# A decoder block's expert layer: 160 instead of 128 of 512 tokens by gathered rows, 352 instead of 384 by dense products

## The reference

```python
def peer_ffn(xn, wq, sub_keys, u, v):          # xn: 512 tokens x 2048
    q = (xt @ wq).reshape(t, 8, 2, 128)        # 8 heads, two half keys
    sc = einsum('thpc,hpnc->thpn', q, sub_keys)
    top_v, top_i = lax.top_k(sc, 16)           # per half key
    ...                                        # best 16 of the 16 x 16 pairs
    expert = take_along_axis(cand_id, best_pos)   # 16 of 16384 experts per head
    gate = softmax(best_v)
    hc = einsum('cd,chkd->chk', xc, u[ec])     # one dot product per chosen expert
    ac = gc * gelu(hc)
    return einsum('chk,chkd->cd', ac, v[ec])   # weighted sum of rows of v
```

## Time and profile before

| what | value |
| --- | --- |
| runs | 3308.53, 3305.33, 6432.45 us; median 3308.53 us |
| profiled execution | 3301.1 us, of which the span from first to last instruction 3299.3 us |
| granted TensorE clock, mean | 0.988 |
| groups of stage 3 | about 1189 to 3076 us of the span |

### The profile page before, as it was taken

How to read it: one execution, slowest core, us unless ns; L and a number is a source line. 1 busy time by engine, 2 the same in 40 slices (tenths; PEclk the granted TensorE clock), 3 DMA queues, 4 the chain that set the end, 5 groups by cost and what they waited for, 6 DMA issues and landing times.

```text
span 3299.3 us, 46895 instructions
## 1 busy us (share of the span) xinstructions
PE 3180.3 (96%) x17074; PEld 2965.8 (90%) x17074; DVE 2431.3 (74%) x3461; ACT 1078.1 (33%) x1379; POOL 659.4 (20%) x464
## 2 busy tenths in 40 slices
PE   7999999999997879999999999999999999999997
PEld 5777778899997779999999999999999999999785
DVE  6544443599977968888887888888888888885644
ACT  4224422222233533333333333333332333333422
POOL 3120000066673111112111121111212111110200
PEclk9999999999998999999999999999999999999998
DMA  4243122344566668888788887888878788863322
GB/s 147 81 153 111 67 84 94 105 112 112 114 187 216 232 238 286 291 285 302 266 291 287 279 306 265 293 282 279 302 270 297 277 286 291 283 238 117 102 90 100
DMA packets 249394, 694.46 MB, mean 210 GB/s; under 512 B 35824, under 2 KB 93680, under 8 KB 213360
## 3 DMA queue, kind: packets, MB, share of 16 engines
q1 hardware_dynamic: 189424, 418.77, 37.0%
q0 software_dynamic: 55296, 268.53, 24.0%
q10 hardware_dynamic: 4608, 6.29, 0.5%
HBM read 657.79 MB, written 35.72 MB: 210 GB/s over the span
## 4 chain that ended last, share of the span: by engine, by line
PE 73%; DVE 16%; DMA 4%; issue 4%; ACT 2%; POOL 1%; DVEq 0%; SPq 0%; ACTq 0%
PE bank L486 23%; PE bank L488 23%; PE bank L487 23%; DVE w_lo L1203 4%; DMA raw<-in_u_t 3%; DVE one_ij L1548 2%; DMA raw<-in_v 1%; ACT w_hi L875 1%; DVE row L1526 1%; PE bank L578 1%; PE bank L601 1%; PE bank L579 1%; POOL gate_matrix L1790 1%; DVE x_lo L1659 1%; DVE x_lo L1220 1%
## 5 line engine op out<-in xcount | busy, mean ns | idle before, releaser
L486 PE MATMUL bank<-x_hi,w_hi 128*128 128x384 f32 (+1 forms) x3024 | 1079.8, 357 | 35.8 <-DVE x_lo L1220 16.7
L488 PE MATMUL bank<-x_hi,w_lo 128*128 128x384 f32 (+1 forms) x3024 | 1069.9, 354 | 0.0
L487 PE MATMUL bank<-x_lo,w_hi 128*128 128x384 f32 (+1 forms) x3024 | 1069.8, 354 | 0.0
L875 ACT ACTIVATE w_hi<-raw 128x1024 fp32r<-128x1024 f32 (+1 forms) x668 | 688.3, 1049 | 887.7 <-DMA raw<-in_v 336.7
L1203 DVE TENSOR_TENSOR w_lo<-raw,w_hi 128x1024 fp32r<-128x1024 f32 (+1 forms) x668 | 802.9, 1219 | 210.0 <-ACT w_hi L875 200.3
L486 PE MATMUL bank<-a_hi,w_hi 128*128 128x384 f32 x2048 | 687.6, 336 | 14.3 <-DVE w_lo L1203 11.1
L487 PE MATMUL bank<-a_lo,w_hi 128*128 128x384 f32 x2048 | 685.8, 335 | 0.0
L488 PE MATMUL bank<-a_hi,w_lo 128*128 128x384 f32 x2048 | 685.8, 335 | 0.0
L486 PEld LDWEIGHTS bank<-x_hi,w_hi 128*128 128x128 f32 x3024 | 571.4, 189 | 85.4 <-DVE w_lo L1203 16.8
L487 PEld LDWEIGHTS bank<-x_lo,w_hi 128*128 128x128 f32 x3024 | 571.9, 189 | 38.8 <-issue 1.2
L488 PEld LDWEIGHTS bank<-x_hi,w_lo 128*128 128x128 f32 x3024 | 571.0, 189 | 38.9
(11 more groups left out here) (198 smaller groups left out, 2049.5 us busy)
## 6 DMA issues: line engine op xcount, KB each, us to landing
raw<-in_u_t SPq DMA_DIRECT2D x256, 512.0 KB
raw<-in_v SPq DMA_DIRECT2D x256, 512.0 KB
g_tile<-gate_matrix SPq DMA_DIRECT2D x32, 768.0 KB
raw<-in_w_o SPq DMA_DIRECT2D x32, 512.0 KB
raw<-in_w_q SPq DMA_DIRECT2D x32, 512.0 KB
gate_matrix<-g_blk SPq DMA_DIRECT2D x8, 2048.0 KB, 7.4
raw<-in_w_gate SPq DMA_DIRECT2D x32, 512.0 KB
raw<-in_w_in SPq DMA_DIRECT2D x26, 512.0 KB
```

The lines of the kernel that those rows point to most:

```text
L486: pe.matmul(out, w_hi[slot][:, blk, :], m_hi, start=first, stop=False)
L487: pe.matmul(out, w_hi[slot][:, blk, :], m_lo, start=False, stop=False)
L488: return pe.matmul(out, w_lo[slot][:, blk, :], m_hi, start=False, stop=last)
L875: act.activation(w_hi[slot][:, 8 * s:8 * s + n, :], raw[s][:, 0:n, :], ACT.Copy)\
```

## The change

TD becomes 352 and the unit of tokens in `x2_hi` and `x2_lo` becomes 32 instead of 128 (TK), so that dense products read 11 pieces of 32 tokens instead of 3 of 128. Tokens 352 to 383 get row buffers of another shape: 32 tokens are spread over the partitions four times, and each copy takes two of the eight heads, so 32 loads of 1 MB bring their rows of `u` and 32 those of `v`. There are 160 dots and 160 mixes in place of 128 each (ALL_ROWS). ALONE becomes 12, ONE_TB 7. Per group there are 12 rows in groups 0 and 1, and 10 (PER_G) in all others up to 29; the added ones stand at the end of quarters 1 and 3 (of all four quarters in groups 0 and 1).

`row_acc` now is the memory of `x_rows`, and so is cleared, by POOL, only when all dots are done. The activations for the rows are made from `h` by ACT and transposed by PE (`rows_stage`, `sparse_rows`) after the first unit of the ALONE stage; those of the spread tokens are made in group 0. At the end 16 small matmuls with a `fold` matrix add the four copies.

```diff
-TD = 384
-TCD = TD // P
+TD = 352
+TCD = TD // P + 1
+TK = 32
-ALONE = 11
+ALONE = 12
-PER_G = 8
-G_DOT = (ROWS - EARLY) // PER_G
+PER_G = 10
+ROWS_B = TK
+ALL_ROWS = ROWS + ROWS_B
+G_DOT = (ALL_ROWS - EARLY) // PER_G
-        x2_hi = at("x2_hi", two, [P, TC, DC, P], F32R)
+        x2_hi = at("x2_hi", two, [P, NPC, DC, TK], F32R)
-        row_acc = at("row_acc", one + 35 * K, [P, D])
+        row_acc = x_rows
+        x_rows_b = at("x_rows_b", one + 35 * K, [P, D])
+        row_acc_b = x_rows_b
...
+        def b_parts(g):
+            return range(4) if g < 2 else (1, 3)
...
             def sparse_rows(i):
-                    pe.matmul(out, x2_hi[:, TCD, 4 * i + j, :], ident_r[:, :], start=True, stop=False)
-                    mm = pe.matmul(out, x2_lo[:, TCD, 4 * i + j, :], ident_r[:, :], start=False, stop=True)
+                for n in (2 * i, 2 * i + 1):
+                    pe.wait_ge(stage_ready, n + 1)
...
+                        mm = pe.transpose(bank[6 + i % 2][:, k * P:(k + 1) * P], stage[n % 2][:, j, :], ident[:, :])
+            def fold_acc_b():
+                pe.wait_ge(acc_added, 3)
+                for c in range(DC):
+                    mm = pe.matmul(bank[6][:, c * TK:(c + 1) * TK], row_acc_b[:, c * P:(c + 1) * P], fold[:, :],
+                                   start=True, stop=True)
...
                 if e == 5:
...
+                    act.wait_ge(topk_step, PER_TOPK * PH)
+                    for q in range(4):
+                        act.dma_start(expert_b[ts, :], ...).then_inc(expert_b_in, 16)
+                        act.dma_start(gate_rows_b[ts, :], ...).then_inc(expert_b_in, 16)
...
             def peer_group(g, par, first=False, last=False):      # ACT
                 if first:
                     hi(peer_unit(g, 1), peer_slot(1, par))
+                    rows_stage_b(0)
+                    rows_stage_b(1)
...
+                    rows_evict_b(0)
+                    rows_evict_b(1)
+                    rows_stage_b(2)
+                    rows_stage_b(3)
...
                 dve.scalar_tensor_tensor(of_head(expert), i_of[:, TCD, :], float(NK), j_of[:, TCD, :], ...)
+                dve.scalar_tensor_tensor(of_head(expert_c), i_of[:, TCD - 1, :], float(NK), j_of[:, TCD - 1, :], ...)
...
                         if c == 1:                                # DVE, quarter q of a group
                             rows(3 + q)
+                        if c == 3:
+                            rows_b(q)
...
-            dve.memset(row_acc[:, :], 0.0).then_inc(acc_zero, 1)
...
-            for k in range(EARLY, 2 * ROWS):                      # POOL
-                load_row(k)
+            for g in range(G_DOT):
+                load_group(g, EARLY + 8 * g, 4 * g if g < 2 else 4 + 2 * g, u_rows)
+            pool.wait_ge(row_done, ALL_ROWS)
+            pool.memset(row_acc[:, :], 0.0).then_inc(acc_zero, 1)
+            pool.memset(row_acc_b[:, :], 0.0).then_inc(acc_zero, 1)
+            for g in range(G_DOT, N_GROUPS - 2):
+                load_group(g, 8 * (g - G_DOT), 2 * (g - G_DOT), v)
```

More of the change, by code:

```diff
@@ L126, in build_block @@
         ident_r = at("ident_r", rest + 17 * K, [P, P], F32R)
-        rinv_col = at("rinv_col", rest + 17 * K + 512, [P, 2])
+        rinv_col = at("rinv_col", rest + 17 * K + 512, [P, 4])
+        stage = [at("stage0", rest + 16 * K, [P, 2, P]), at("stage1", one + 60 * K + 512, [P, 2, P])]
+        fold = at("fold", rest + 17 * K + 576, [P, TK])
+        expert_c = at("expert_c", rest + 17 * K + 704, [P, PH, TOPK], U32)
+        expert_b = at("expert_b", rest + 18 * K + 192, [P, ROWS_B], U32)
+        gate_rows_b = at("gate_rows_b", rest + 18 * K + 320, [P, ROWS_B])
+        dots_b = at("dots_b", rest + 18 * K + 448, [P, ROWS_B])
+        mix_b = at("mix_b", rest + 18 * K + 576, [P, ROWS_B])
         z = at("z", h_at, [P, N_IN, T])
@@ L740, in _ @@
             pe.wait_ge(s_ready, 2 * PH - 1)
-            pe.matmul(bank[2][:, 0:2], rinv[:, TD:T], ident[:, 0:2], start=True, stop=True).then_inc(col_made, 1)
-            for e in range(1, 6):
+            pe.matmul(bank[2][:, 0:2], rinv[:, T - P:T], ident[:, 0:2], start=True, stop=True)
+            pe.wait_ge(stage_ready, 9)
+            pe.matmul(bank[2][:, 2:4], stage[0][:, 0, :], ident[:, 0:2], start=True, stop=True).then_inc(col_made, 1)
+            for e in range(2, 6):
                 alone(e)
@@ L1048, in _, with rows_stage @@
             score_out(2 * PH - 1, 1)
+            def rows_stage(n):
+                if n >= 2:
+                    act.wait_ge(stage_used, n - 1)
+                for j in range(2):
+                    c = 2 * n + j
+                    ins = act.activation(stage[n % 2][:, j, :], h[:, c, T - P:T], ACT.Copy,
+                                         scale=gain[:, c + G_FFN - C_GAIN:c + G_FFN - C_GAIN + 1])
+                ins.then_inc(stage_ready, 1)
             def rows_evict(i):
-                act.wait_ge(rows_made, i + 1)
+                act.wait_ge(stage_used, 2 * i + 2)
                 act.activation(x_rows[:, 4 * P * i:4 * P * (i + 1)], bank[6 + i % 2][:, :], ACT.Copy).then_inc(rows_out, 1)
@@ L1096, in _, with rows_stage_b, rows_evict_b @@
                     g_block(2 * b2 + s, s)
-            for s in range(2):
-                act.wait_ge(g_stored[s], 16 * (ONE_TB // 2 - 1))
-                g_block(ONE_TB - 2 + s, s, last=s == 1)
+            act.wait_ge(g_stored[0], 16 * (ONE_TB // 2))
+            g_block(ONE_TB - 1, 0, last=True)
+            def rows_stage_b(i):
+                if i >= 2:
+                    act.wait_ge(stage_b_used, i - 1)
+                for j in range(4):
+                    c = 4 * i + j
+                    ins = act.activation(stage_b[i % 2][:, j, :].rearrange("p (q t) -> p q t", t=TK),
+                                         h[:, c, TD:TD + TK].unsqueeze(1).to_broadcast([P, 4, TK]), ACT.Copy,
+                                         scale=gain[:, c + G_FFN - C_GAIN:c + G_FFN - C_GAIN + 1])
+                ins.then_inc(stage_b_ready, 1)
+            def rows_evict_b(i):
+                act.wait_ge(stage_b_used, i + 1)
+                act.activation(x_rows_b[:, 4 * P * i:4 * P * (i + 1)], bank[6 + i % 2][:, :], ACT.Copy).then_inc(rows_out, 1)
             def gelu(j):
@@ L1149, in _ @@
             for s in range(2):
[L1150 removed]
+                act.wait_ge(g_stored[s], 16 * ((ONE_TB + 1 - s) // 2))
             peer_group(0, 0, first=True)
@@ L1227, in _ @@
             dve.tensor_copy(ident_r[:, :], ident[:, :]).then_inc(consts_done, 1)
+            dve.tensor_reduce(fold[:, :], ident[:, :].rearrange("p (q t) -> p t q", t=TK), AX.X, ALU.add)\
+               .then_inc(fold_made, 1)
             rope = [0]
@@ L1569, in _ @@
                 for s in range(2):
-                    g_block(2 * b2 + s, s, loads=b2 + (EARLY - ONE_TB) // 2 + 1)
+                    g_block(2 * b2 + s, s, loads=b2 + (EARLY - ONE_TB + s) // 2 + 1)
+            g_block(ONE_TB - 1, 0)
             def scale(j, m, par, n, u=None, b=None):
```

224 lines of the change are left out of this document (157 added, 67 removed).

## The result

3462.1 us median (3453.2 to 3468.2, four runs) against 3306.9 before: a ratio of 1.047, 95% interval 1.045 to 1.049. The ratio leaves out one run of the kernel before that took 6432.5 us. The changed kernel is slower, where I forecast 3323 and no change that counts; my range ended at 3385.

What follows compares the result with a forecast made beforehand. PE bounds stage 3 before, DVE after. Terms 25 + 4 + 5 + 0.7 - 16.4 + 8 - 2.5 - 2 give +22 us on the profiled 3301.1: 3323 us, range 3275 to 3385.

Steps and rivals of the forecast that it cites:

- PE's pitch: Dense matmuls in stage 3: 352 columns take 0.160 us each instead of 0.1733, so PE asks 53.8 us a group.
- Rival E: PE's moving operand in 11 pieces of 32 costs cycles; 512-wide gate units at the end take 5 to 10 us; chance 0.03.
- Rival C: PE's clock falls after idle time ahead of quarter 0, costing 1.8 us a group, 3373 us if not hidden; chance 0.05.
- What late weights add on top decides: Stage 3 groups: of 2.2 us late weights the added row absorbs 1.3; 0.9 stay, plus 0.5 for traffic.
- My 57.65 for DVE's chain: Groups 2 to 29: DVE's chain of 54.3 us, plus 4.45 for two added rows, less 1.1 for narrower operations.
- Rival B: DMA paces groups from quarter 3 to the next group's third `lo`: 61.0 us a group, 3376 us; chance 0.11.
- A: Late weights vanish in stage 3 and DVE's chain alone paces a group at 57.6 us, 3278 us; chance 0.16.
- D: DVE isn't the bound, as ACT exchanges aren't fixed; stage 3 goes at PE's 53.8 us, 3175 us; chance 0.03.
- Groups 0 and 1: Four added rows each, less waits: +5 us for group 0 and +4 us for group 1.
- The start of the blocks: First one-hot tile waits for dot 8 and its load, 3.3 us later; the added dense unit fits in PE's idle time.
- The turn: From dots to mixes: POOL clears two buffers before issuing a load, so DVE stands longer, +8 us (5 to 11).
- Group 30: No rows, PE-bound: -4.5 us, about 2 back for 16 fold matmuls and a fifth addition, so -2.5 us.

## Why the prediction was wrong

**PE's pitch and the clock.** I forecast 0.160 us; over `a_hi` and `a_lo` it is 0.161, but over `x2` in its 11 pieces of 32 it is 0.164, so PE asks 144 x 0.164 + 192 x 0.161 = 54.5 us a group, not 53.8, and 54.6 is what the run with two raw buffers and no added rows took with dots. Rival E named this; it cost stage 3 nothing, and at the end, where 768 matmuls over 512 columns take it in 16 pieces, the pitch is 0.235 us against 0.226:

```profile
3300.15 0.40 PE L512 MATMUL bank<-x_hi,w_hi 128*128 128x512 f32 x1
3300.39 0.40 PE L513 MATMUL bank<-x_lo,w_hi 128*128 128x512 f32 x1
3300.62 0.40 PE L514 MATMUL bank<-x_hi,w_lo 128*128 128x512 f32 x1
```

768 x 0.009 = 7 us, by E's own count 5 to 10: right size, and with my -2 for group 31 it covers the +5.0 behind the groups. Rival C's cause is there too:

```profile
1527.06 0.66 PE L512 MATMUL bank<-x_hi,w_hi 128*128 128x352 f32 x1 [2.69 <-DVE w_lo L1306]
1527.52 0.49 PE L513 MATMUL bank<-x_lo,w_hi 128*128 128x352 f32 x1
1527.81 0.49 PE L514 MATMUL bank<-x_hi,w_lo 128*128 128x352 f32 x1
1528.11 0.49 PE L512 MATMUL bank<-x_hi,w_hi 128*128 128x352 f32 x1
```

Eleven matmuls 0.29 us apart, the 1.2 GHz level, after a stop of 2.69 us: 1.4 us. From 1400 to 3000 us there are 26 such pieces, about one a group, each close behind a stop of 1.8 us or more; other stops as long have none. The mean clock of the stretch is 0.97, against 1.00 before. It cost the changed kernel next to nothing, since DVE and ACT hardly waited for PE (8.3 us in 25 groups). By the Trainium skill (TensorE: Matmul & The Clock Gate, Part 1) idleness takes the clock back; the trace agrees in that every such piece stands behind a stop.

**"What late weights add on top decides": the sentence was right, the number failed, and this is the step that made the forecast wrong.** I took the 2.2 us of late weights in the earlier trace rows for a property of the loads, let the added row absorb 1.3 and added 0.5 for traffic. But they were measured while PE paced the group. With one raw buffer a unit is asked for when the one before is split, so its landing and ACT's copy stand between two splits. PE's pace of 58.2 us hid most of that; when PE's time fell below it, it came out. The pairs show it: with the dense cut alone 3.8 us are late, and 0.6 once there is a second buffer; with the added rows 5.0, and 0.2 once there is a second buffer. Why the added rows bring 1.2 more isn't shown: taking away their data, or their operations, or moving them didn't bring it back. My 57.65 for DVE's chain then holds: 57.0 with dots, 58.05 with sums. The step that failed is the one that kept a wait's size when the engine that hid it was about to stop hiding it.

**Rival B** gave 3376, 86 us short of the result, and the right place, quarter 3 to the third `lo`. Its sign came too: the weights for the second `lo` landed later than 7.7 us after they were asked for (8.4 and some 11). But its reason, a ceiling of the queues, fell: the second buffer moves the same bytes, in fewer microseconds. One stretch of 10 us in the run with filled gaps moved 416 GB/s. The Trainium skill (HBM Reference, Specifications (TRN2)) gives about 358 GB/s as a core's share when both cores stream, and about 425 for a core alone; the trace agrees with the second:

```profile
1440.00:1450.00 10.00, 10.00 (x63) 10.00 (x62) 6.90 (x13) 5.34 (x8) 0.98 (x1) 1.00 1.02 416
```

What traffic does is to lengthen a landing, and without row data the lateness is 0.9. The loss needs both: long landings and a single buffer. Rivals A and D are refuted for this kernel; A's 57.6 is what the second buffer reaches.

**Groups 0 and 1**, +17.7 for +9. The same cause for the larger part: with two raw buffers they take 64.2 and 61.6, +7.8.

**The start of the blocks**, +9 for +3.3:

```profile
1021.03 2.29 DVE L1633 SCALAR_TENSOR_TENSOR row<-row,x_rows 128x2048 f32<-128x2048 f32 x1
1023.24 2.29 DVE L1633 SCALAR_TENSOR_TENSOR row<-row,x_rows 128x2048 f32<-128x2048 f32 x1
1030.90 2.29 DVE L1633 SCALAR_TENSOR_TENSOR row<-row,x_rows 128x2048 f32<-128x2048 f32 x1 [5.37 <-DMA row<-in_u_rows,expert]
1033.12 2.29 DVE L1657 TENSOR_TENSOR one_ij<-iota,hk_t 128x2048 f32<-128x2048 f32 x1
```

```profile
1023.60 2.74 POOL L1957 DMA_INDIRECT row<-in_u_rows,expert  x1 [6.72 <-DVE row L1633]
```

"The dense unit fits where PE stands idle" counted PE alone. Its split stands in DVE's order ahead of the dots (at 1021.03, the dot that frees a row buffer), so the last row is asked for at 1023.60 and not at 1019.06, and lands 7.3 us later. That ACT's eight issues hold a copy was seen (969.98 to 975.40, and DVE waited 4.01), where I had let it pass for nothing.

**The turn**: +12.5 for +9, of which 4.5 are what every group lost; the rest is the forecast 8. The waits are 3.6 us for the memset and 6.3 for row loads.

**Group 30**, -2.5 forecast; the two periods from group 29 to group 31 gave +9.5:

```profile
3110.52 1.72 PE L825 MATMUL bank<-ident,x_rows 128*128 128x128 f32 x8 [2.71 <-DVE h L1714]
3114.33 7.04 PE L832 MATMUL bank<-fold,x_rows_b 128*128 128x32 f32 x32 [2.09 <-DVE h L1714]
```

```profile
3121.40 0.69 DVE L1721 TENSOR_TENSOR h<-bank,h 128x512 f32<-128x512 f32 x1 [6.53 <-PE bank L832]
...
3130.81 0.53 DVE L1692 TENSOR_TENSOR h_s<-bank,rinv 128x352 f32<-128x352 f32 x1 [6.45 <-PE bank L514]
```

The fold's 16 matmuls (two records each) take 7.04 us where I had 2 with the addition. DVE waits 6.53 us for them with the next split queued behind the addition, and so PE's next unit starts late and DVE waits 6.45 where it had waited 2.83: an added wait is paid again when the awaited engine needs what is queued behind it.

## What to carry to other kernels

A wait measured under one bound is no estimate of it under another: before an edit shortens the pacing engine, add up the loop of each single-buffered tile (asked for, landed, copied, split, asked for again) and see whether it is shorter than the new pace. Where it isn't, try a second buffer before any order: here it was worth 162 us, while the orders tried with one buffer (the rows' place, the gate tile, all three together) gave between +47 and -49, and cuts of the added rows' data and operations at most -73. Only leaving those rows and their places out altogether (-154), or all row data (-133), did as much, and neither computes the layer. Once the loads are ahead, gaps in the bound engine's order (0.56 us behind each gelu) are real time: filling three of them a group gave 49 us. On the kernel before, where PE sets the pace, the same edit gave nothing.
